# Moving the last three input projections of a mixer among its attention items

## The reference

```python
h = h + 0.5 * rms_norm(swiglu(rms_norm(h, g[0]), ffn1...), g[1])
m = hybrid_mixer(rms_norm(h, g[2]), ...)      # three head groups side by side
h = h + rms_norm(m, g[3])
h = h + 0.5 * rms_norm(swiglu(rms_norm(h, g[4]), ffn2...), g[5])

# in hybrid_mixer
proj = u @ w_in
qa, ka, va, us, qc, kc, vc, fc = split(proj)
ya = swa_sink_attention(qa, ka, va, ...)      # 8 heads, window of 128
yb = s5_mixer(us, ...)                        # state space, gelu, glu
yc = fox_attention(qc, kc, vc, fc, ...)       # 4 heads, causal over all 512
y = concatenate([rms_norm(ya, ga), rms_norm(yb, gb), rms_norm(yc, gc)])
return y @ w_out
```

## Time and profile before

| | us |
|---|---|
| median of 3 runs | 1960.92 |
| lowest and highest run | 1959.69, 1961.51 |
| the profiled execution | 1955.62 |
| its span, first to last instruction | 1953.8 |
| TensorE busy | 1926.2 (99%) |
| VectorE busy | 1123.0 (57%) |
| ScalarE busy | 876.5 (45%) |
| GpSimd busy | 223.2 (11%) |

### The profile page before, as it was taken

How to read it: one execution, slowest core, us unless ns; L and a number is a source line. 1 busy time by engine, 2 the same in 40 slices (tenths; PEclk the granted TensorE clock), 3 DMA queues, 4 the chain that set the end, 5 groups by cost and what they waited for, 6 DMA issues and landing times.

```text
span 1953.8 us, 25457 instructions
## 1 busy us (share of the span) xinstructions
PE 1926.2 (99%) x9136; PEld 1555.5 (80%) x9136; DVE 1123.0 (57%) x1585; ACT 876.5 (45%) x1390; POOL 223.2 (11%) x422
## 2 busy tenths in 40 slices
PE   8999999999999999999999999999999999999998
PEld 7788888877767788888878888887876778888887
DVE  5785553287657655553277755335876576555423
ACT  5554432264654544442255544323566455444321
POOL 2851000013100000000048010000131000000000
PEclk9999999999999999999999999999999999999999
DMA  6334343342213333343333443333502123333331
GB/s 176 104 103 130 95 121 89 82 143 80 55 44 87 94 94 101 91 122 93 91 97 97 130 107 109 106 92 99 158 27 65 54 79 98 101 91 107 113 89 43
DMA packets 330956, 188.56 MB, mean 97 GB/s; under 512 B 6996, under 2 KB 325432, under 8 KB 329848
## 3 DMA queue, kind: packets, MB, share of 16 engines
q1 hardware_dynamic: 324008, 168.13, 29.8%
q0 software_dynamic: 5824, 18.79, 3.4%
q10 hardware_dynamic: 1040, 0.52, 0.1%
HBM read 175.72 MB, written 11.67 MB: 96 GB/s over the span
## 4 chain that ended last, share of the span: by engine, by line
PE 89%; DVE 5%; ACT 4%; issue 2%; DMA 1%; POOL 0%; DVEq 0%; ACTq 0%; POOLq 0%
PE ps L549 17%; PE ps L550 16%; PE ps L551 16%; PE ps L686 8%; PE ps L685 8%; PE ps L684 8%; PE ps L577 2%; PE ps L578 2%; PE ps L582 2%; PE ps L886 2%; PE ps L834 1%; ACT wh L1013 1%; PE ps L861 1%; DVE wl L1472 1%; PE ps L842 1%
## 5 line engine op out<-in xcount | busy, mean ns | idle before, releaser
L1472 DVE TENSOR_TENSOR wl<-raw,wh 128x1024 fp32r<-128x1024 f32 (+1 forms) x270 | 357.9, 1326 | 527.1 <-ACT wh L1013 525.8
L549 PE MATMUL ps<-xh,wh 128*128 128x512 f32 x1552 | 612.1, 394 | 4.5 <-DVE wl L1472 4.5
L551 PE MATMUL ps<-xh,wl 128*128 128x512 f32 x1552 | 605.6, 390 | 0.0
L550 PE MATMUL ps<-xl,wh 128*128 128x512 f32 x1552 | 605.3, 390 | 0.0
L1013 ACT ACTIVATE wh<-raw 128x1024 fp32r<-128x1024 f32 (+1 forms) x270 | 304.9, 1130 | 437.8 <-PE ps L686 331.3
L549 PEld LDWEIGHTS ps<-xh,wh 128*128 128x128 f32 x1552 | 292.0, 188 | 75.2 <-DVE wl L1472 9.2
L551 PEld LDWEIGHTS ps<-xh,wl 128*128 128x128 f32 x1552 | 291.9, 188 | 61.9
L550 PEld LDWEIGHTS ps<-xl,wh 128*128 128x128 f32 x1552 | 292.2, 188 | 58.4
L684 PE MATMUL ps<-Hh,wh 128*128 128x512 f32 x704 | 274.0, 389 | 0.0
L686 PE MATMUL ps<-Hh,wl 128*128 128x512 f32 x704 | 273.9, 389 | 0.0
L685 PE MATMUL ps<-Hl,wh 128*128 128x512 f32 x704 | 273.9, 389 | 0.0
(11 more groups left out here) (313 smaller groups left out, 2035.5 us busy)
## 6 DMA issues: line engine op xcount, KB each, us to landing
raw<-in_ffn_up SPq DMA_DIRECT2D x88, 512.0 KB, 3.8
raw<-in_ffn_down SPq DMA_DIRECT2D x64, 704.0 KB, 4.6
raw<-in_ffn_gate SPq DMA_DIRECT2D x87, 512.0 KB, 3.8
raw<-in_w_in SPq DMA_DIRECT2D x28, 512.0 KB, 4.0
raw<-in_w_out SPq DMA_DIRECT2D x16, 512.0 KB, 3.9
xrow<-in_x SPq DMA_DIRECT2D x2, 1024.0 KB, 8.5
ssm_t<-evict POOLq DMA_DIRECT2D x8, 256.0 KB, 3.1
ssm_v<-evict POOLq DMA_DIRECT2D x8, 256.0 KB, 2.7
```

Source lines behind the costliest of these rows:

```text
L549: pe.matmul(bank, w_tile(True, slot, kw), xh[:, kx, :], start=first, stop=False)
L550: pe.matmul(bank, w_tile(True, slot, kw), xl[:, kx, :], start=False, stop=False)
L551: return pe.matmul(bank, w_tile(False, slot, kw), xh[:, kx, :], start=False, stop=last)
L1472: V.tensor_tensor(w_low(slot, k0, nk), raw[:, slot4, 0:nk - k0, :], w_high(slot, k0, nk).bitcast(F32), ALU.subtract).then_inc(w_split, 1)
```

## The change

The last three projections move: `kc1` from items 12 and 13 to 13 and 14, then `qc1` in items 17 and 18 and `vc1` in items 21 and 22, where before `vc1` stood in items 16 and 17 and `qc1` in items 19 and 20. The low half of the weights of the last tile moves from item 15 to 16. The second FoX value tile is turned in item 24, not 20, into bank 7 in place of 6, and waits for VectorE to have read the gate's logits from that bank. The branch sum in bank 6 waits only for the value tile before. The split of the output projection's tile 1 moves from item 22 to 23 on ScalarE, and its low half from 23 to 24 on VectorE.

```diff
-        ("vc0", VC0), ("kc0", KC0), ("qc0", QC0), ("kc1", KC0 + P), ("vc1", VC0 + P), ("qc1", QC0 + P)]
+        ("vc0", VC0), ("kc0", KC0), ("qc0", QC0), ("kc1", KC0 + P), ("qc1", QC0 + P), ("vc1", VC0 + P)]
...
-        VT_BANK = (4, 6, 6)
+        VT_BANK = (4, 6, 7)
...
                     if v == 2:
 
-                        pe.wait_ge(v_rdy, l * 3 + v)
+                        pe.wait_ge(gl_lg, (l + 1) * 2)
...
                     if b == 0:
 
-                        pe.wait_ge(v_rdy, (l + 1) * 3)
+                        pe.wait_ge(v_rdy, l * 3 + 2)
...
-OUT_SPLIT_AT = {21: 0, 22: 1, 30: 2, 31: 3}
+OUT_SPLIT_AT = {21: 0, 23: 1, 30: 2, 31: 3}
...
-LOW_AT = {3: 11, 8: 12, 12: 13, 15: 14}
-PROJECT_AT = {0: 9, 4: 10, 8: 11, 12: 12, 16: 13, 19: 14}
-VALUES_AT = (None, 8, 20)
+LOW_AT = {3: 11, 8: 12, 12: 13, 16: 14}
+PROJECT_AT = {0: 9, 4: 10, 8: 11, 13: 12, 17: 13, 21: 14}
+VALUES_AT = (None, 8, 24)
```

## The result

The changed kernel took 1962.68 us (median of 18 runs, 1960.72 to 1965.27) against 1959.57 us (18 runs, 1954.62 to 1961.51). The recorded ratio is 1.0025, 95% interval 1.0019 to 1.0031, or 4.9 us slower. It is not the quotient of these two medians, which lie 3.1 us apart; the means of the same runs lie 4.0 us apart. The change is slower by each of the three, and its size is known to 1 or 2 us. The forecast was +4.4 us. The profiled execution of the changed kernel took 1962.69 us and has a span of 1960.9 us.

A forecast was written before the change was run, and what follows sets the result against it. TensorE, busy 99% of the span, was taken as the bound. New stalls of 5.1 us a layer against 2.9 removed gave +2.2 a layer, +4.4 us over two layers: 1965.3 us from a median of 1960.92, range 1960.5 to 1970.0.

The forecast's parts named there:

- Item 12: Without its half projection, turn waits for VectorE's probabilities and attend for ScalarE's copy: 1.7 us a layer, bounds 1.2 to 1.8.
- Item 16: No projection there any more; turn waits 0.8 for VectorE, attend 0.45 for ScalarE: 1.2 us a layer, bounds 0.3 to 1.7.
- Item 20: Projection gone from items 19 and 20; turn waits 0.2, attend 0.5: 0.7 us a layer, bounds 0 to 1.2.
- Item 25: Moved split delays ScalarE's copy that turn(22) needs: 1.5 us lost where 1.15 were, bounds 0.6 to 2.0.
- The waits of items 22 and 24: Three late waits, covered by the half projection now in item 22: a gain of 1.8 us a layer.
- Item 17's wait on the transfer: Wait before the gate's product in layer 1, 0.3 us, claimed to stay; at best it goes.
- The clock: TensorE's granted clock claimed to stay at 1.00 throughout; a fall in item 13 would show the forecast wrong.
- rival (1): Clock falls once in each layer, about 4 us long, costing 1.9: +8.2 us, 1969.1 us; chance 0.25.
- edits at nothing: Later value turn in item 24, its new and dropped waits, and ScalarE's later tile copy claimed to cost nothing.

The follow-up runs named there:

- The second experiment: Changed kernel with kc1's projection put back in items 12 and 13, the other two projections as changed; ratio 1.0039 to the kernel before.
- The first: Changed kernel with the split of output tile 1 put back in item 22; ratio 1.0015 to the kernel before.
- the other three with fillers: Fillers in: changed kernel with kc1 back in item 12, 1.0011; changed kernel with only vc1 late, 0.9997; kernel before, 0.9986.
- the three in their good places: Changed kernel, split 1 in 22, projections in 12, 16, 20: 0.9971; projections and splits as before: 0.9976; first one with split 0 in 20: 0.9961.
- the late part with fillers: Changed kernel with kc1 and qc1 in items 12 and 16, only vc1 late in 21, fillers in items 20 and 25; ratio 0.9997.
- the order alone: Changed kernel keeping only the tiles' order, later value turn and its bank; projections and splits as in the kernel before; ratio 0.9976.

## Why the prediction was right, and where it was not

**The waits, term by term**, start to start, a layer. Item 12: 1.7 forecast, 1.11 and 0.42 of idle shown, 1.8 with the 0.13 to 0.16 that each row leaves out. Item 16: 1.2 forecast, 0.61 and 0.42 shown, about 1.3. (By the forecast's own numbers the turn of item 16 would wait 0.6, from 1474.7 to 1473.5 + 1.81, and not the 0.8 written; it waited 0.75.) Item 20: 0.7 forecast, 0.49 shown and a turn that starts at 1497.20 behind a mask product at 1496.92, 0.2 late, so 0.8. Item 25: 1.5 forecast, 1.39 of idle shown, 1.5. The waits of items 22 and 24 are gone. That is 5.4 us a layer in place of 5.1, and layer 0's stretch with the clock held grew by 2.36 us where +2.2 was forecast. Item 17's wait on the transfer, 0.35 us in layer 1, is gone too. The forecast had kept it; but it is also absent from the second profile of the kernel before, so its going is not shown to be the change's doing. The forecast sum was +4.4 us; the stretches with the clock held gave +4.35. That they agree to 0.05 us is luck: without the transfer's wait on either side it is +4.7. The mechanism is the one that was forecast, and each term lies within its bounds, item 12's at the upper end. The timelines of VectorE and ScalarE before the change were enough for it, since neither moved in items 11 to 13.

**What each wait hangs on.** The second experiment settles that item 12's wait is not a cost of its own but an advance on item 16's: the late chain is worth the same wherever the hole is. The first settles what the split does in item 25: 0.7 us of the wait, and VectorE's probabilities stand right behind it.

**The clock.** This step was wrong. The forecast held that the clock stays at 1.00 throughout, and named as a sign of its being wrong that it falls in item 13. It fell there, in layer 1 (0.66 from 1465 to 1470), and behind item 25 in layer 0. The stretches of the changed kernel's profile grew by 7.7 us, which is the path of rival (1), given at +8.2 us and a chance of 0.25. I had argued against it that the late items of the kernel before keep the full clock. That row was one execution. The second profile shows a fall at this very place, and fillers make the kernel before 2.7 us faster. The changed kernel's own falls can be put the same way: 4.9 measured, less 4.35 for its waits, plus the 2.7 that the kernel before loses, about 3 us; in its own profile the falls make 3.3 (117.36 less 114.02). Both kernels lose about 3 us to the clock, each known to some 2 us, and that nearly cancels in their difference. So the number came out near +4.4 for two reasons: its sum of waits was right, and a term of about 3 us that it put at nothing stands on both sides. The second is luck.

Over the other kernels the same account holds. Ratio times 1958 us, less the change of the stretches with the clock held, leaves the gain of having no falls: -2.2 for the changed kernel with fillers, -1.8, -2.4 and -2.6 for the other three with fillers, -1.9, -3.1 and -2.4 for the three in their good places (-5.7 less -3.8, -4.7 less -1.6, -7.6 less -5.2). Each is uncertain by some 2 us, and taken one by one only those of the late part with fillers, of the kernel before with fillers and of the order alone are clearly away from zero. That the kernels without fillers had no falls in most executions was seen in their one profile each, and is otherwise argued. One kernel shows how little one profile says: with the split back in item 22 there was no fall in the stretches, yet the rest is 0.0 (2.9 less 3.0), so most of its executions must have had them.

A rival to part of this was not tested. The fall behind line 629 comes once, twice or not at all in an execution, and the parts outside the stretches took from 1842.9 to 1847.3 us in the 13 profiles. If an edit changes how often that happens, some of these 2 to 3 us belong there. The run by run times of the kernel before with and without fillers speak for the stretches, but do not exclude it.

The Trainium skill ("TensorE: Matmul & The Clock Gate", section "A second HAM failure mode: psum-queue depth-cycling") says that frequent short idle times between groups of matmuls make the clock swing. The prediction left open whether that holds here. The falls inside the stretches agree with it, in both kernels (0.66 and 0.91 above); those behind line 629, with no idle time in front of them, are not of its kind.

**What failed outright** was "edits at nothing". The order of two tiles and the place of one turn took 1.3 us of late waits from each layer and added 0.5 in item 19, 0.8 net. I had costed them only by what TensorE issues and by whether their new wait is met. What they take from VectorE and ScalarE in front of a late wait (0.7 and 0.5 us) I had not counted as a gain, nor the later release of bank 1 as a cost. That the changed kernel holds the same gain, hidden by where its projections stand, is argued and was not run apart.

## What to carry to other kernels

A piece of matrix work placed between two steps of a chain on other engines is cover; before moving it, read when each step's releaser ends on its own engine, since the next wait is the difference and not zero, and a hole filled in one item may only open in the next. Count what an edit takes from the engines that release the waits as well as what it takes from the bound one. Where several short holes lie close together, take a second profile before calling the clock held: whether it falls differs from execution to execution, and filler products in the hole test it directly. When a profile is set against a median, see first which of the kernel's executions it is, and add up the parts that no edit touches as well.

## What the runs showed of the hardware

The granted clock fell behind short waits. In the changed kernel TensorE had waited 1.11 and 0.42 us within 2.2 us, and had done two small groups of products between, when in layer 1 the next scores and the projection ran slow; in layer 0 the same pair of waits left the clock at 1.00. In the kernel before, the fall stood behind waits of 0.44 and 0.99 us in items 24 and 25, in one layer of the four that two executions show. A fall cost 1.6 to 1.7 us (18.29 to 19.90 us for items 12 to 16; 22.37 to 24.04 and 17.69 to 19.27 for items 21 to 27), and more where it lasted longer: 2.5 us behind the 1.64 us wait (55.62 to 58.13 us for the stretch of layer 0) and 2.8 behind the 2.16 us wait in layer 1 (56.82 to 59.58). During a fall 128x512 matmuls follow each other in 0.43 us and not 0.23 to 0.24, which is the lower of the two levels, 1.2 and 2.4 GHz. 12 to 20 filler products of 0.18 us a layer held it in all eight stretches that have them.

It also fell where TensorE had not waited at all. The 64 products of line 629 (64x16, 3.75 us at full clock, one every 0.06 us) stand in a row of work without a pause. Behind or within them the clock fell in layer 0 in all 13 profiles and in layer 1 in 11, not in the first of the kernel before nor in the order alone. The part between the stretches took 906.1 to 906.2 us without the fall in layer 1, 907.5 to 907.8 with it, and 909.3 where it lasted twice as long. What decides between two executions with equal work stayed open in both cases.
